# Four edits at stage boundaries of a two-layer streaming encoder: value weights, mixer squares, sample states, last projection tile

## The reference

```python
# layer 0: heads normed, gated, projected; state per stream is an output
o_dn  = _rmsnorm(o_dn, dn_onorm)   * silu(dn_gate)      # 8 heads x 64
o_gla = _rmsnorm(o_gla, gla_onorm) * silu(gla_gate)     # 8 heads x 64
x = x + concatenate([o_dn, o_gla]) @ w_out              # 1024 x 1024
# layer 1
q, k, v = split(_rmsnorm(x, c_norm) @ c_w_qkv, 3)       # v: 1024 columns
x = x + attention(q, k, v) @ c_w_out
x = x + swiglu(_rmsnorm(x, ffn_norm))
```

## Time and profile before

| | |
|---|---|
| three runs | 3695.6, 3708.3, 3709.0 us (median 3708.3) |
| profiled execution | 3698.2 us, its span 3696.5 us |
| mean granted TensorE clock | 0.930 of full speed |
| TensorE (PE) busy | 3358.9 us, 91% of the span |
| VectorE (DVE), GpSimd (POOL), ScalarE (ACT) busy | 35%, 30%, 20% |
| mixer stage starts, next one starts | 1012.1, 1180.4 us |
| key projection's last copy, value stage starts | 2244.9, 2249.9 us |
| last matmul of `project_add`, next stage starts | 2819.2, 2829.0 us |

### The profile page before, as it was taken

How to read it: one execution, slowest core, us unless ns; L and a number is a source line. 1 busy time by engine, 2 the same in 40 slices (tenths; PEclk the granted TensorE clock), 3 DMA queues, 4 the chain that set the end, 5 groups by cost and what they waited for, 6 DMA issues and landing times. The chain is left out here.

```text
span 3696.5 us, 63238 instructions
## 1 busy us (share of the span) xinstructions
PE 3358.9 (91%) x26808; PEld 3140.3 (85%) x26808; DVE 1285.8 (35%) x1705; ACT 728.4 (20%) x1292; POOL 1107.2 (30%) x701
## 2 busy tenths in 40 slices
PE   5979968888658999999998997899988999999997
PEld 5968847777558999999998996666678999999997
DVE  3630033555455333333333110055532333333333
ACT  4321131232122100000101100166622000000003
POOL 4442032443061332223224233011133323232223
PEclk7989966888779999999999998899999999999999
DMA  4222120110151111111110223365611111111101
GB/s 152 85 85 93 48 64 22 42 36 34 33 187 46 46 36 55 40 40 34 41 50 12 84 93 124 114 176 146 170 44 46 46 51 40 40 34 46 51 28 51
DMA packets 269354, 246.41 MB, mean 67 GB/s; under 512 B 23624, under 2 KB 234145, under 8 KB 269176
## 3 DMA queue, kind: packets, MB, share of 16 engines
q1 hardware_dynamic: 262040, 217.49, 18.6%
q0 software_dynamic: 7136, 26.35, 2.4%
HBM read 191.77 MB, written 54.13 MB: 67 GB/s over the span
## 5 line engine op out<-in xcount | busy, mean ns | idle before, releaser
L285 PE MATMUL PS<-hT_high,w_split_tiles 128*128 128x384 f32 x5376 | 1088.1, 336 | 16.4 <-POOL w_split_tiles L299 11.0
L285 PEld LDWEIGHTS PS<-hT_high,w_split_tiles 128*128 128x128 f32 x5376 | 949.6, 189 | 16.8 <-POOL w_split_tiles L299 11.2
L285 PE MATMUL PS<-hT_low,w_split_tiles 128*128 128x384 f32 x2688 | 613.1, 335 | 0.0
L285 PE MATMUL PS<-ffn_act_split,w_down_split 128*128 128x384 f32 x3024 | 530.1, 335 | 4.9 <-issue 4.9
L285 PEld LDWEIGHTS PS<-ffn_act_split,w_down_split 128*128 128x128 f32 x3024 | 526.8, 188 | 5.2 <-issue 5.2
L285 PEld LDWEIGHTS PS<-hT_low,w_split_tiles 128*128 128x128 f32 x2688 | 482.0, 189 | 0.0
L690 DVE TENSOR_TENSOR xT<-xT,PS 128x1152 f32<-128x1152 f32 x168 | 227.4, 1354 | 300.9 <-PE PS L285 300.9
L271 PE MATMUL PS<-w_rest_split,hT_high 128*128 128x512 f32 x576 | 177.4, 389 | 0.0
L466 POOL CAST w_split_tiles<-w_raw_tiles 128x1024 fp32r<-128x1024 f32 x44 | 47.0, 1067 | 391.5 <-PE PS L285 321.3
L466 POOL CAST w_split_tiles<-attention_oT 128x1024 fp32r<-128x1024 f32 x42 | 43.7, 1041 | 342.0 <-PE PS L285 333.2
L285 PE MATMUL PS<-hT_high,w_conv_split 128*128 128x384 f32 x576 | 125.0, 343 | 4.8 <-issue 4.8
(11 more groups left out here) (398 smaller groups left out, 4803.2 us busy)
## 6 DMA issues: line engine op xcount, KB each, us to landing
w_raw_tiles<-in_ffn_w_gu_dram SPq DMA_DIRECT2D x44, 512.0 KB, 3.9
attention_oT<-in_ffn_w_gu_dram SPq DMA_DIRECT2D x44, 512.0 KB, 3.8
cache_k<-in_cache_c_k_dram SPq DMA_DIRECT2D x64, 256.0 KB, 5.6
cache_v<-in_cache_c_v_dram SPq DMA_DIRECT2D x64, 256.0 KB, 5.0
ffn_room<-in_ffn_w_down_dram SPq DMA_DIRECT2D x11, 1024.0 KB, 5.9
attention_oT<-in_ffn_w_down_dram SPq DMA_DIRECT2D x11, 1024.0 KB, 5.9
rest_dram<-rest_rows SPq DMA_DIRECT2D x36, 256.0 KB, 2.1
qk_dram<-qk_cols SPq DMA_DIRECT2D x16, 576.0 KB, 2.8
```

The source lines that it names most:

```text
L285: m = nc.tensor.matmul(PS[:, banks + j, 0:GN], wl if p == 2 else wh, sl if p == 1 else sh, start=(n == 0 and p == 0), stop=(n == last and ...
```

## The change

1. **`project_add`.** The adds of squares move from GpSimd to VectorE. The eighth column tile is multiplied group by group (`multiply_last`), and VectorE's add, ScalarE's square and VectorE's add of squares follow for each group of 384 tokens. The loops of TensorE and VectorE over the tiles are partly or wholly written out.
2. **`recurrences`.** SyncE issues the six stores of sample states behind the store of the second tile, before that turn's load.
3. **`mixer_out`.** ScalarE squares the rows; tile 1 has a second buffer for its squares, in the unused end of `xT`. The gate is no longer multiplied with the head gains; they are one column for each half of the heads (features lie on partitions after the turn) and scale the high part on ScalarE and the low part on VectorE. GpSimd has only the weights' low parts left. Four small loads of gains stand behind the first tiles' loads instead of two ahead of them, and SyncE's last load of `xT` waits for the sums of tile 1. ScalarE's order at the start changes.
4. **`qkv_projection` and `v_projection`.** The first half of the value weights is loaded and split in the stage before, in buffers of its own: two loads at its start, two pieces split ahead of each of the last two tile splits. `v_projection` splits only the second half, into the freed buffers of the tile weights and one new one.

```diff
 # project_add
             for n in range(KT):
                 split_tile(e, pool, n // 2, n % 2, raw, ws, w_in, mm, high, split)
-                if n >= 4:
-                    add_square(n - 3)
             split_next(0)
-            add_square(KT - 3)
             split_next(1)
-            add_square(KT - 2)
-            add_square(KT - 1)
...
+            def multiply_last():
+                pe.wait_ge(split, KT)
+                pe.wait_ge(added, KT)
+                for j in range(G):
+                    for k in range(KT):
+                        for p in range(3):
+                            m = nc.tensor.matmul(PS[:, 3 + j, 0:GN], ws[:, 1, int(p == 2), k], parts(pair)(k, j)[int(p == 1)],
+                                                 start=(k == 0 and p == 0), stop=(k == KT - 1 and p == 2))
+                    m.then_inc(mm if j == G - 1 else mm_part, 1)
...
+            for n in range(KT - 1):
+                dve.wait_ge(mm, n + 3)
+                b = 3 * (n % 2)
+                nc.vector.tensor_tensor(groups(xT[:, n]), groups(xT[:, n]), PS[:, b:b + G, 0:GN], ALU.add).then_inc(added, 1)
+                if n > 1:
+                    add_square(n - 1)
+            add_square(KT - 2)
+            for j in range(G):
+                dve.wait_ge(mm if j == G - 1 else mm_part, KT + 2 if j == G - 1 else j + 1)
+                x = xT[:, KT - 1, j * GN:(j + 1) * GN]
+                nc.vector.tensor_tensor(x, x, PS[:, 3 + j, 0:GN], ALU.add).then_inc(added, 1)
+                dve.wait_ge(squared, KT + j)
...
 # recurrences
                     sp.dma_start(e.scr["o"][order[s] * P:(order[s] + 1) * P], ob[:, s % 2]).then_inc(o_out[s % 2], 16)
+                if s == 1:
+                    sample_states_out()
                 if n is not None and n + 1 < NT:
                     load(n + 1)
...
 # mixer_out
-            for t in tiles(0):
-                square(t)
-                gain_gate(t)
             for n in range(KT):
                 w_rest(n)
-            for j in range(G):
-                if j + 1 < G:
-                    for t in tiles(j + 1):
-                        square(t)
-                        gain_gate(t)
...
+            def square_o(t):
+                act.wait_ge(o_in[slot(t)], 16 * load_of(t))
+                if t >= 2:
+                    act.wait_ge(summed, 1 if t == 2 else t)
+                nc.scalar.activation(sq_at(t), o_at(t), ACT.Square).then_inc(squared, 1)
...
-                    copy(oT_half(hi, t, h), turned_bank(t, h)).then_inc(high, 1)
+                    nc.scalar.activation(oT_half(hi, t, h), turned_bank(t, h), ACT.Copy, scale=gain[:, h:h + 1]).then_inc(high, 1)
...
+            square_o(0)
+            square_o(1)
             root(0)
+            square_o(2)
             root(1)
+            root(2)
+            act.wait_ge(gain_in, 16 * 4)
             high_part(0)
-            root(2)
+            w_first(0)
             high_part(1)
-            w_first(0)
             w_first(1)
             high_part(2)
...
                     if j + 1 < G and n in (0, 2, 4):
+                        square_o(tiles(j + 1)[n // 2])
                         root(tiles(j + 1)[n // 2])
...
-                    tt_(oT_half(lo, t, h), turned_bank(t, h), oT_half(hi, t, h), ALU.subtract).then_inc(low, 1)
+                    v.scalar_tensor_tensor(out=oT_half(lo, t, h), in0=turned_bank(t, h), scalar=gain[:, h:h + 1],
+                                           in1=oT_half(hi, t, h), op0=ALU.mult, op1=ALU.subtract).then_inc(low, 1)
...
 # qkv_projection, GpSimd
+            def split_v(n):
+                k = slice(2 * n, 2 * n + 2)
+                pool.wait_ge(v_in[n], 16)
+                nc.gpsimd.tensor_copy(wv_first[:, 0, k], vraw[:, n % 2]).then_inc(v_high, 1)
+                pool.wait_ge(v_high, n + 1)
+                nc.gpsimd.tensor_tensor(wv_first[:, 1, k], vraw[:, n % 2], wv_first[:, 0, k], ALU.subtract).then_inc(v_low, 1)
+                if n + 2 < KT // 2:
+                    pool.wait_ge(v_low, n + 1)
+                    load_v(n + 2)
+            load_v(0)
+            load_v(1)
...
             for s in range(2):
+                split_v(2 * s)
+                split_v(2 * s + 1)
                 split_tile(e, pool, NB // 2 - 1, s, wraw, ws, w_in, mm, w_high, w_low, 1)
...
 # v_projection, TensorE
-                    if t == 0 and k % 2 == 0:
-                        pe.wait_ge(w_low, j * KQ + k // 2 + 1)
+                    if j and t == 0 and k % 2 == 0:
+                        pe.wait_ge(w_low, k // 2 + 1)
```

More of the change, by code:

```diff
@@ L783, in _ @@
         def _(pool):
-            def add_square(n):
-                pool.wait_ge(squared, n + 1)
-                if n > 1:
-                    pool.wait_ge(sq_added, n - 1)
-                nc.gpsimd.tensor_tensor(row[:], row[:], sq[:, n % 2], ALU.add).then_inc(sq_added, 1)
             def split_next(n):
@@ L834, in _ @@
                 nc.scalar.activation(sq[:, n % 2] if n else row[:], xT[:, n], ACT.Square).then_inc(squared, 1)
+            act.wait_ge(sq_added, KT - 3)
+            for j in range(G):
+                act.wait_ge(added, KT + 2 + j)
+                c = slice(j * GN, (j + 1) * GN)
+                nc.scalar.activation(sq[:, 1, c], xT[:, KT - 1, c], ACT.Square).then_inc(squared, 1)
         @block.vector
@@ L2248, in mixer_out @@
         x_in = [e.sem(ctx, f"x_in{n}") for n in range(KT)]
[L2249 removed]
+        (gain_in, eps_set, squared, summed, rooted, inverted, normed, gated, turned, high, low, w_high, w_low,
          mm, added, x_squared, sq_added) = e.sem(
             ctx, "head_gain_in", "o_eps_set", "o_squared", "o_summed", "o_rooted", "o_inverted", "o_normed",
[L2252 removed]
+            "o_gated", "o_turned", "oT_high", "oT_low", "w_high", "w_low", "out_mm", "out_added", "x_squared",
             "x_sq_added")
@@ L2713, in _ @@
                 for k in range(KT):
-                    if t == 0 and k % 2 == 0:
-                        pe.wait_ge(w_low, j * KQ + k // 2 + 1)
-                    m = rows_split(nc, PS[:, n % 4, :], hT, t, w[:, j], k, k == 0, k == KT - 1)
+                    if j and t == 0 and k % 2 == 0:
+                        pe.wait_ge(w_low, k // 2 + 1)
+                    c = slice(t * P, (t + 1) * P)
+                    w, at = (second[k // KQ], k % KQ) if j else (w_first, k)
+                    for p, (h, x) in enumerate(((0, 0), (0, 1), (1, 0))):
+                        m = nc.tensor.matmul(PS[:, n % 4, :], hT[h][:, k, c], w[:, x, at], start=(k == 0 and p == 0),
+                                             stop=(k == KT - 1 and p == 2))
                 m.then_inc(mm, 1)
```

109 lines of the change are left out of this document (58 added, 51 removed).

## The result

The changed kernel took **3648.3 us** (median of four runs, 3637.8 to 3661.0), the kernel before 3705.1 beside it (four runs, 3695.6 to 3709.0). The ratio is **0.985**, with a 95% interval of 0.9825 to 0.988: faster by 1.5%, where 0.5% can be told from no change. The forecast was 3649 us, with a range of 3635 to 3670. The profiled execution of the changed kernel took 3642.3 us, its span of 3640.4 us is 56.1 shorter than before; the sum of the prediction was 55.1.

A forecast was written before the change was run, and what follows sets the result against it. TensorE, busy 91% of the span, was taken as the bound, so only its standstills count. 5.3 + 5.9 + 3.0 + 19.7 + 21.2 = 55.1 us off the mean 3704.3 gave 3649 us, range 3635 to 3670.

The forecast's parts named there:

- D: Value projection: TensorE no longer waits for GpSimd's weight splits at the start; 21.2 us saved (18.0 to 21.7).
- The cover in the key projection: Key projection: GpSimd idled 9.4 us before the last tile split, so the moved value-weight splits cost nothing.
- Rival 2: Key projection: late value-weight loads delay GpSimd's tile splits; 45 us gained in all, 3659 us; chance 0.07.
- C1: Start of the mixer: first product ready 30.4 us into the stage instead of 32.6; 3.0 us taken (2.2 to 4.2).
- C2: Inside the mixer: stall after two products 2.0 us instead of 12.7, later stalls nearly gone; 19.7 us saved (10 to 22).
- Rival 1: Mixer: ScalarE becomes the queue that holds tiles up; some 39 us gained in all, 3665 us; chance 0.15.
- Rival 3: Mixer: a table load per switch between squares and roots; 32 us gained in all, 3672 us; chance 0.03.
- B: End of the recurrences: six sample-state store issues no longer delay the prompt states' stores; 5.9 us saved (5.4 to 6.6).
- the cost is nothing: Recurrences: moved stores hide in SyncE's idle time, the load behind them having 29 us of cover; otherwise up to 6.4 us.
- A: End of the attention projection: GpSimd's split becomes last instead of its adds of squares; 5.3 us saved (3.5 to 5.3).
- Rival 4: Whole kernel: TensorE, with fewer pauses, is granted a lower clock; time 3704 to 3725 us; chance 0.04.

The follow-up runs named there:

- hold experiment: The changed kernel with GpSimd's first weight split of the mixer held until tile 2 is gated: ratio 0.9867, mixer 142.4 us.
- c_only: The kernel before with the mixer edit (change 3) alone: median 3676.1 us, ratio 0.9931, mixer 144.0 us.

## Why the prediction was right, step by step

*D, 21.2 forecast, 21.8 measured.* The first copy came 7.6 us after the stage's start (forecast 8.2, 2258.1 - 2249.9). The measured gain is just over the 21.7 called "at best", because the profile of before is the longest of its kind: from the last key copy to the first value copy the seven profiles without D took 32.5 to 34.4 us (mean 33.2), so D is worth 19.9 to 21.8 there, 20.6 against the mean. The cover in the key projection held: 1.17 us of idle time are left, and the last split, done at 2194.1, is wanted when the product before it ends, at 2203.8. Rival 2 looked at the right place, since the second pair of pieces stands directly ahead of that split, and no load came late enough to use the cover up.

*C1, 3.0 forecast, 2.4 measured: a mis-sized term.* The chain that was worked out ends at 30.4 us, and 30.2 was measured, but by two errors against each other. Tile 0 was squared at 3.7 us and not at 6.6, so tile 2's multiplies began at 19.9 in place of about 22.6. They gave it back: taken at 2.1 us each beside GpSimd, from the first row of VectorE in the earlier trace rows, they took 3.3. The nearest row was a multiply beside squares and gains; the operation that it would now meet was a subtraction of two large operands. The hold experiment puts the whole collision at 4.1 us. The gains in the high and low parts cost what was allowed for them: 0.68 us for a half in place of 0.59, and 0.75 in place of 0.69.

*C2, 19.7 forecast, 22.1 measured: a mis-sized term.* It lies above the forecast's "22 if no stall is left", although a stall is left. From the first product to the last matmul are 111.1 us (1040.94 to 1152.0), forecast 113.4. The first two products took 11.4 (10.8), the wait 2.5 (2.0), and the rest 97.1, which is the forecast's 97.6 of matmuls and turns at full clock. The 0.5 of later waits and the 2.5 of half-clock running did not come: with no pause over the stretch the granted clock was 1.00 throughout. A part of the 22.1 is the profile of before: against the mean of six unchanged mixers the stage as a whole became 23.6 us shorter and not 24.5, still more than the 22.7 forecast. Rival 1, ScalarE as the queue, fell; GpSimd's reordered queue in the kernel before showed that the 12.7 us were one position in an in-order queue. Rival 3, a table load for each switch, fell with the one load in the trace. The Trainium skill, ScalarE: Activation LUTs, section Table sets: the hidden batching unit, counts a load for each change of set; the trace agrees in so far as nine squares and nine roots of the rows, mostly in turn, have one load between them, so Square and Sqrt are in one set here.

*B, 5.9 forecast: the step at the end right, 6.07 measured, and "the cost is nothing" not shown.* Of the 6.07, 5.3 are the earlier start of the prompt states' stores behind the last row store, and 0.8 their quicker issue (3.5 us, before 4.2). The moved stores took 7.1 us of issuing where they now stand, 0.7 more than at the end, SyncE issued the load at 687.96, and nothing waited for it by name. But the recurrences became 1.4 us shorter, not 5.9. Of the 4.6 us difference 1.5 lay ahead of the moved stores and so are not B's; of the rest, 1.8 to 2.5 us go with B in the comparison of fourteen profiles, but that B causes them is not shown. Its net worth is then near 4 us if it does, 6.1 if it doesn't, and which it is stays open. The prediction took the recurrences' other turns as fixed; they are not. The stage differed by 2.6 us between two profiles of the kernel before, by 3.8 between two of the changed kernel, and by 10.5 on one chip between kernels that don't differ in it (513.7 to 524.2).

*A, 5.3 forecast, 5.0 measured.* As forecast, the split became the last work, and the next start follows it by 0.9 us (2773.04 to 2773.93). The 0.3 us are the split itself, 2.68 beside VectorE's last pieces (2.35 before). VectorE's last add of squares took 0.56, not 1.0.

That the total came within 1 us is luck. In this pair of profiles 1.8 in the mixer, 1.6 in the value stage, 0.4 in the last stretch and 1.9 in the attention stage, which no edit touches, came on top and met the 4.5 that the recurrences did not give; most of these are the spread of the stages between executions. What the trace of before could settle, the place and the order of the ends, was right in all four, and this is what the forecast is to be credited with. Rival 4, the clock, did not come in the long stages: the feed-forward of layer 0 took 850.3 us in both.

## What to carry to other kernels

Where engines run their queues in order, ask of each wait whose queue it stands in and what stands behind it: taking the work off GpSimd's queue, with the rest of change 3, removed some 24 us; moving one item of it forward gained 5 to 9, with a new wait of 7.3 one turn later; and a wait added on GpSimd came out as 11.4 us on TensorE by way of SyncE's loads. When an edit is worth less than the spread of the runs, measure it at its own place, between two events in the trace. Repeat the profile of both kernels before putting down a difference elsewhere to it, and compare a stretch that the edit can't have touched: if that differs as much, the difference isn't yet the edit's. Work that is hidden by idle time is free only while the pair of engines doesn't slow each other, so price it with a row where both run the kinds of operation that will meet.

## What the runs showed of the hardware

VectorE's multiplies of two SBUF operands (128x1024) took 1.22 us alone and 2.58 to 3.30 beside GpSimd's subtraction, which went from 2.35 to 2.8 each. The two together are nearly serial: two multiplies and two subtractions need 2.4 + 4.7 = 7.1 us one after the other, and took 6.7 (1030.55 to 1037.27). The Trainium skill, SBUF — State Buffer, section SBUF: two separate sides, says that a VectorE operation with two inputs in SBUF and a GpSimd operation that reads SBUF take one pair of ports in turn, each for its whole length. The traces agree with that, but for the 0.4 us by which the four came out shorter than in series. Sums over one operand, at 1.22, and VectorE's additions from PSUM, at 0.55, took as long beside GpSimd as alone.

The granted clock of TensorE in the recurrences, a stage of small matmuls with waits between, is not fixed by the kernel: from the first row store to the second it was 0.73 and 0.77 in two profiles of one program, and the stretch took 60.65 and 56.46 us. The mixer of the kernel before, with its five waits, was granted 0.95 to 0.98 behind the longest of them and took 165.0 to 169.5 us. In the changed mixer, behind its only wait, it was 1.00 in both profiles of the changed kernel and in c_only, and the stage repeated to 0.1 us; where this wait was 3.89 us instead of 2.54, it was 0.91 for the first 19.4 us.

Tile 0's rows were used 3.7 us after the stage's start, 3.7 us after their load was issued; in the kernel before they were used after 7.5, of which 0.9 went to issuing two gain loads and 6.6 passed from their own issue. c_only, with the old end of the recurrences, has 3.8, so the moved stores aren't the reason. What else is, no run takes apart.
